# Norm scales on the weights, one norm fewer, the forget rows as a bias, and a re-planned state-space core in a four-layer decoder block

## The reference, cut to what matters

```
h = x
h = even_layer(h, mem)        # 8 heads differential attention, gated conv, 4 heads over mem
h = odd_layer(h, mem)         # 12 heads forgetting attention (C), 4 heads over mem (X)
h = h + s5_mixer(rms_norm(h, a_norm), ...);  h = h + conv_ffn(rms_norm(h, ffn_norm[0]), ...)
k, v = shared_kv(h, kv_norm, ...)            # rms_norm(h, kv_norm) @ w_kv
h = h + sb_mixer(rms_norm(h, b_norm), k, v, ...);  h = h + conv_ffn(rms_norm(h, ffn_norm[1]), ...)

def rms_norm(x, g):  return x * rsqrt(mean(x * x, -1) + EPS) * g
# forgetting attention, per head: s = q @ k.T * scale + cum[query] - cum[key], causal; softmax; @ v
#   cum = cumsum(log_sigmoid(u @ w_f + b_f)) per head
# s5_mixer: u = xn @ w_in; y = state-space scan of u; y = y + d_skip * u; gelu(y) @ w_glu, gated
```

## Time and profile before

| | |
|---|---|
| median of 3 runs | 2669.84 us (2668.22 to 2670.76) |
| the profiled execution, its own time | 2668.6 us |
| its span | 2666.8 us |
| mean granted TensorE clock | 0.944 of full speed |
| busy: PE, PEld, DVE, ACT, POOL | 2428.4 (91%), 1905.4 (71%), 1380.5 (52%), 921.4 (35%), 267.7 us (10%) |
| HBM read, written | 212.69 MB, 23.07 MB (88 GB/s) |

### The profile page before, as it was taken

How to read it: one execution, slowest core, us unless ns; L and a number is a source line. 1 busy time by engine, 2 the same in 40 slices (tenths; PEclk the granted TensorE clock), 3 DMA queues, 4 the chain that set the end, 5 groups by cost and what they waited for, 6 DMA issues and landing times.

```text
span 2666.8 us, 29121 instructions
## 1 busy us (share of the span) xinstructions
PE 2428.4 (91%) x10950; PEld 1905.4 (71%) x10950; DVE 1380.5 (52%) x2819; ACT 921.4 (35%) x1408; POOL 267.7 (10%) x314
## 2 busy tenths in 40 slices
PE   4789989799599999999889989999989899899998
PEld 3667667578477676766678768887868646688877
DVE  6875565746545353534454344444443585455543
ACT  3334434332443434342321332223333464322232
POOL 6541000024001010100000000000010231000000
PEclk9889999899799999999885999999989799899999
DMA  6344112125222121213263223332322101223222
GB/s 173 105 146 127 64 48 80 32 79 174 63 79 65 62 66 61 72 55 115 98 203 109 95 76 95 101 103 73 103 72 87 48 1 48 64 95 95 95 80 95
DMA packets 191360, 233.46 MB, mean 88 GB/s; under 512 B 39456, under 2 KB 120823, under 8 KB 191223
## 3 DMA queue, kind: packets, MB, share of 16 engines
q1 hardware_dynamic: 170503, 211.05, 24.9%
q10 hardware_dynamic: 20719, 20.56, 2.5%
HBM read 212.69 MB, written 23.07 MB: 88 GB/s over the span
## 4 chain that ended last, share of the span: by engine, by line
PE 84%; DVE 8%; issue 3%; ACT 3%; SPq 1%; DMA 1%; ACTq 0%; POOL 0%; DVEq 0%; POOLq 0%
PE G L1771 23%; PE G L1773 22%; PE G L1772 22%; PE X L1858 2%; PE X L1924 2%; PE X L1959 2%; PE X L1876 1%; ACT w_hi L991 1%; PE X L1829 1%; PE X L1780 1%; PE X L1843 1%; PE G L1866 1%; PE X L1846 1%; PE X L1817 1%; PE X L1842 1%
## 5 line engine op out<-in xcount | busy, mean ns | idle before, releaser
L1411 DVE TENSOR_TENSOR w_lo<-raw,w_hi 128x512 fp32r<-128x512 f32 x696 | 483.7, 737 | 606.4 <-ACT w_hi L991 606.1
L1771 PE MATMUL G<-w_hi,u_hi 128*128 128x512 f32 x1600 | 650.8, 407 | 21.9 <-issue 14.8
L1773 PE MATMUL G<-w_hi,u_lo 128*128 128x512 f32 x1600 | 632.0, 395 | 0.0
L1772 PE MATMUL G<-w_lo,u_hi 128*128 128x512 f32 x1600 | 631.3, 395 | 0.0
L991 ACT ACTIVATE w_hi<-raw 128x2048 fp32r<-128x2048 f32 (+1 forms) x176 | 333.8, 1897 | 825.4 <-PE G L1773 790.1
L1771 PE MATMUL G<-u_hi,w_hi 128*128 128x512 f32 x1120 | 450.5, 402 | 0.0
L1772 PE MATMUL G<-u_lo,w_hi 128*128 128x512 f32 x1120 | 441.6, 394 | 0.0
L1773 PE MATMUL G<-u_hi,w_lo 128*128 128x512 f32 x1120 | 441.0, 394 | 0.0
L1771 PEld LDWEIGHTS G<-w_hi,u_hi 128*128 128x128 f32 x1600 | 306.1, 191 | 106.6 <-issue 35.1
L1773 PEld LDWEIGHTS G<-w_hi,u_lo 128*128 128x128 f32 x1600 | 305.2, 191 | 66.8
L1772 PEld LDWEIGHTS G<-w_lo,u_hi 128*128 128x128 f32 x1600 | 306.0, 191 | 61.3 <-issue 0.5
(11 more groups left out here) (271 smaller groups left out, 2373.6 us busy)
## 6 DMA issues: line engine op xcount, KB each, us to landing
raw<-in_ffn_w_up SPq DMA_DIRECT2D x88, 512.0 KB, 4.7
raw<-in_e_w_in SPq DMA_DIRECT2D x56, 512.0 KB, 4.8
raw<-in_o_w_in SPq DMA_DIRECT2D x56, 512.0 KB, 4.6
raw<-in_ffn_w_down SPq DMA_DIRECT2D x40, 512.0 KB, 4.5
raw<-in_e_w_out SPq DMA_DIRECT2D x16, 512.0 KB, 4.6
raw<-in_o_w_out SPq DMA_DIRECT2D x16, 512.0 KB, 4.2
raw<-in_a_w_glu SPq DMA_DIRECT2D x16, 512.0 KB, 4.1
raw<-in_w_kv SPq DMA_DIRECT2D x16, 512.0 KB, 4.3
```

Source lines behind the costliest of these rows:

```text
L1411: V.tensor_tensor(w_lo[:, n % HL, k], raw[:, n % RAW, k], w_hi[:, n % HL, k].bitcast(F32), ALU.subtract).then_inc(w_lo_done, 1)
L1771: pe.matmul(out, lh, rh, start=start, stop=False)
L1772: pe.matmul(out, lh, rl, start=False, stop=False)
L1773: return pe.matmul(out, ll, rh, start=False, stop=stop)
```

## The change

1. **Scales on the weights.** For the 124 units behind a norm, `w_high` becomes four ACT instructions of 128x512 with a scale operand, each with its own count, and `w_low` four `scalar_tensor_tensor` instead of `tensor_tensor`, each waiting for its own piece. `u_hi` and `u_lo` lose the scale. The first `w_high` waits for the scale vectors. The 12 forget columns are multiplied by `o_norm` once.
2. **The second norm stage** (`b_norm`, `again=1`) is gone: the q chunks use the rows made for `kv_norm`.
3. **Forget rows.** `cum` is stored to DRAM once; each head's line is loaded back spread over 128 partitions into one of three buffers `c_row` (three loads by SP, nine by ACT, one behind the last exponential of a head). The matmul L1843 and DVE's `row` are gone. The query tiles run from i = 3 down to 0; before each, POOL sets the part of `c_row` above the diagonal to -3e38 (48 `affine_select` of 128x128), waiting for the maximum of the tile before; DVE's maximum reads `c_row` in place of `bias_tile` and waits for POOL.
4. **S5 core.** `d_skip` goes into the prepared matrices (32 small matmuls and 8 ACT copies more in `prep`), DVE's L1574 is gone. u and y are loaded back in pairs (72 transfers in place of 128), the scan has eight output buffers and y four, and the slots of V, Y, gelu and `u_lo` are re-planned.

```diff
-                nc.scalar.activation(w_hi[:, n % HL, 0:kn], raw[:, n % RAW, 0:kn], ACT.Copy).then_inc(w_hi_done, 1)
+                if unit_gain[n] is None:
+                    nc.scalar.activation(w_hi[:, n % HL, 0:kn], raw[:, n % RAW, 0:kn], ACT.Copy).then_inc(w_hi_done, 1)
+                    return
+                name, k0 = unit_gain[n]
+                for k in range(4):
+                    nc.scalar.activation(w_hi[:, n % HL, k], raw[:, n % RAW, k], ACT.Copy, scale=gain(name, k0 + k))\
+                        .then_inc(w_hi_done, 1)
...
+                        dve.wait_ge(w_hi_done, hi_before[n] + k + 1)
+                        V.scalar_tensor_tensor(w_lo[:, n % HL, k], raw[:, n % RAW, k], gain(name, k0 + k),
+                                               w_hi[:, n % HL, k].bitcast(F32), ALU.mult, ALU.subtract)\
+                            .then_inc(w_lo_done, 1)
...
-        plan_norm("h", "b_norm", again=1)
...
+            s.steps = [(hd, TT - 1 - i if kind == "C" else i) for hd in range(heads) for i in range(TT)]
...
+                if n == forget.n + 3:
+                    sp.wait_ge(*at_("cum_done", forget.i))
+                    sp.dma_start(dC, cum).then_inc(c_sum_stored, 16)
+                    sp.wait_ge(c_sum_stored, 16)
+                    for hd in range(3):
+                        sp.dma_start(c_row[hd], dC[hd].partition_broadcast(P)).then_inc(c_row_loaded[hd], 16)
...
+            def pool_c_rows(s, ts):
+                for t in ts:
+                    hd, i = s.steps[t]
+                    H = s.y0 + hd
+                    d = c_row[H % 3][:, P * i:P * i + P]
+                    if t % TT:
+                        pool.wait_ge(*at_("score", s.i, t - 1))
+                    else:
+                        pool.wait_ge(c_row_loaded[H % 3], 16 * (H // 3 + 1))
+                    pool.affine_select(out=d, in_=d, compare_op=ALU.is_ge, fill=BIG, base=0, pattern=[[-1, P]],
+                                       channel_multiplier=1).then_inc(*by("row_masked", s.i, t))
...
+                                dve.wait_ge(*at_("row_masked", s.i, t))
+                                b = c_row[head % 3][:, 0:L]
...
+                    if s.akind == "C" and is_last(s, t) and H < C_HEADS:
+                        act.dma_start(c_row[H % 3], dC[H].partition_broadcast(P)).then_inc(c_row_loaded[H % 3], 16)
...
-                            pe.matmul(b[:, 0:L], q, att[:, 4 + hd, 0:L], start=True, stop=False)
-                            ins = pe.matmul(b[:, 0:L], ones[0:C_HEADS, :], row[:, 0:L], start=False, stop=True)
+                            ins = pe.matmul(b[:, 0:L], q, att[:, 4 + hd, 0:L], start=True, stop=True)
...
-        S5_V = {2: 0, 3: 1, 4: 2, 5: 3, 7: 4, 8: 5, 9: 6, 10: 7}
-        S5_Y = {6: 0, 7: 1, 8: 2, 9: 3, 10: 4, 11: 5, 12: 6, 13: 7}
-        S5_SKIP = {9: (0,), 10: (1,), 11: (2,), 12: (3,), 13: (4,), 14: (5,), 15: (6, 7)}
-        S5_LOW = {10: (0,), 11: (1,), 12: (2, 3), 14: (4,), 15: (5, 6, 7)}
-        S5_GELU = {10: (0,), 11: (1,), 12: (2,), 13: (3,), 14: (4,), 15: (5, 6, 7)}
+        S5_V = {2: (0,), 3: (1,), 4: (2, 3), 7: (4, 5), 9: (6,), 10: (7,)}
+        S5_Y = {6: (0,), 7: (1,), 8: (2,), 9: (3,), 10: (4,), 11: (5, 6), 13: (7,)}
+        S5_GELU = {10: (0, 1), 11: (2, 3), 14: (4, 5), 15: (6, 7)}
+        S5_LOW = {9: (0, 1), 11: (2, 3), 14: (4, 5), 15: (6, 7)}
...
-                dve.wait_ge(s5_y_loaded[k], 16 * 8)
-                    y = big[:, 8 + k, :]
-                    V.scalar_tensor_tensor(y, big[:, k, :], gain("d_skip", k), y, ALU.mult, ALU.add)\
+                        ins = pe.matmul(b[0:32, g * P:g * P + 16], s5_skip[:, 32 * g:32 * g + 32], s5_fold,
+                                        start=False, stop=True)
```

More of the change, by code:

```diff
@@ L38, in weight_units @@
 def weight_units(w):
-    units = []
+    units, gains = [], []
     def cols(mat, k0, kn, c):
@@ L53, in paired, with chunk @@
                 (v[:, k0:k0 + 4, cb:cb + 256], slice(0, 4), slice(256, 512))]
-    def chunk(mat, c):
+    def chunk(mat, c, norm):
         units.append(cols(mat, 0, 4, c))
         units.append(cols(mat, 4, 4, c))
+        gains.extend([(norm, 0), (norm, 4)])
     def down(mat, kt, first=0):
@@ L95, in weight_units @@
                 units.append(paired(w["ffn_w_up"][layer], k0, DFF + 256 * c, 256 * c))
+                gains.append((f"ffn{layer}", k0))
         down(w["ffn_w_down"][layer], 22)
-    return units
+    return units, gains
 class Stage:
@@ L242, in stage, with plan_norm @@
             return s
[L244 to L251, removed]
+        def plan_norm(src, name, T=TT):
+            s = stage("norm", src=src, name=name, T=T, n=state["n"], h=state.get("h"), y=state.get("y"))
+            for t in range(T):
+                mark("squared", s.i, t)
+            for t in range(T):
+                mark("xn_ready", s.i, t)
             s.aux = [aux("u_ready", s.i, k) for k in range(KT)]
@@ L1110, in act_prep @@
                            .then_inc(s5_p_stored[c], 16)
+                if t == 0:
+                    nc.scalar.activation(s5_skip, ident[:, :], ACT.Copy, scale=gain("d_skip", 0))\
+                        .then_inc(*by("s5_skip", s.i, 0))
                 if t - 1 in PREP_K:
@@ L1118, in act_prep @@
                                          ACT.Copy).then_inc(*by("s5_evac", s.i, i, "k"))
+                    if i + 1 < KT:
+                        nc.scalar.activation(s5_skip, ident[:, :], ACT.Copy, scale=gain("d_skip", i + 1))\
+                            .then_inc(*by("s5_skip", s.i, i + 1))
                     act.wait_ge(*at_("s5_evac", s.i, i, "k"))
@@ L1481, in dve_slot @@
                         .then_inc(*by("score", s.i, t))
-                    if s.akind == "C" and i == TT - 1 and hd < s.heads - 1:
-                        V.tensor_scalar(row, cum, ident[0:C_HEADS, head + 1:head + 2], None, ALU.mult)\
-                            .then_inc(*by("row_ready", s.i, hd + 1))
                 if 1 <= t <= T:
@@ L1619, in _ @@
                         dve.wait_ge(*at_("u_hi_done", s.i, k))
-                        V.scalar_tensor_tensor(u_lo[:, k, 0:P * s.T], X[:, s.aux[k] % 4, 0:P * s.T], gain(s.name, k),
-                                               u_hi[:, k, 0:P * s.T].bitcast(F32), ALU.mult, ALU.subtract)\
+                        V.tensor_tensor(u_lo[:, k, 0:P * s.T], X[:, s.aux[k] % 4, 0:P * s.T],
+                                        u_hi[:, k, 0:P * s.T].bitcast(F32), ALU.subtract)\
                             .then_inc(*by("u_ready", s.i, k))
```

204 lines of the change are left out of this document (106 added, 98 removed).

## The result

The changed kernel takes 2596.16 us (median of 4 runs, 2591.71 to 2603.32) against 2670.3 beside it: a ratio of 0.973, with a 95% interval from 0.970 to 0.975. That is 74 us less. I had forecast 2624.5 with 2600 as the low end: the sign was right, and the gain was 1.6 times as large as forecast and outside the range. The profiled execution was the fastest of the four, 2591.71 us with a span of 2589.5, so span against span the gain is 77.3 us.

The account below looks back on a forecast made before the run. PE, busy 91% of the span, was taken to bound the kernel. The terms summed to -45.1 us, taking the profiled 2668.6 to 2623.5, as a median 2624.7, stated as 2624.5 us; range 2600 to 2642.

Parts of the forecast that it names:

- Part 1: Forgetting attention: without the row matmul its streaming goes, -25.8 us over 12 heads, with +2.5 back in the last group.
- Part 2: Start of each group of forgetting attention: PE's three waits for DVE's `row` go, -6.2 us, and clock loss behind, -3.4.
- Part 3: Second norm: PE's gap between the v chunk and the q chunk goes, -7.2 us, nothing reasonable less than -5.
- Part 4: Weights' split: ACT's longer w_high ahead of eight norms +4.9, PE's waits for DVE -7.2, unscaled u_hi and u_lo -3 us.
- The rival in which part 1 turns into waiting for DVE: Forgetting attention: DVE or the mask loop takes the row matmul's 26 us as waiting; 2650 us, chance 0.05.
- Part 5: Prep: 32 more small matmuls and slower w_lo, less two waits for w_hi; net +1.8 us (-2 to +7).
- Part 7: POOL's 48 masks in forgetting attention: wait hidden, but they run beside DVE's w_lo; +1.5 us (0 to +15).
- Part 6: S5 core: re-planned slots remove one PE wait and lengthen another; -3 us in all (-30 with the clock, to +15).
- rival of stalling pairs: S5 core: u and y of a pair wait for the second tile's store; +15 us, 2639.5, chance 0.10.
- The wait of 4.8: S5 core: PE's second wait for ACT's copy, as ACT stood in gelu(0) needing y0 from DRAM; 4.8 us, to go.
- the first wait: S5 core: PE waits 3.2 us for ACT, which splits a weight unit before copying Y1; stays, +1.7 us.
- the first rival: S5 core: with fewer pauses the clock stays at 2.4 GHz; -20 us, 2604.5, chance 0.12.

## Why the prediction was too small

- **Part 1, the row matmul: the step that failed.** "The other 0.19 I take for the change to the next kind of operand, which stays when q*k stands there instead." It does not stay. The 0.19 belongs to the row matmul's 12 operand rows and goes with it, and so do 0.1 us ahead of it and 0.1 us behind it that the chain of waits had put down to its neighbours: 0.41 us in each of 48 slots, 19.7 us, of the 32 by which the spans moved more than forecast. I had -34.9 as the bound if the 0.19 went too; the true value, 44.6, lies outside even that, since I only looked at what the chain put on the row's own line. The streaming (25.8 forecast, 0.21 us per 128 keys) was right. Of the 2.5 us given back in the last group 1.3 came, and elsewhere: the waits for DVE's scaling there are 4.2 us instead of 4.4, and a wait ahead of a product of the down product is 3.6 instead of 2.1.
- **Part 2** held for the waits (6.2, all gone). Taking the wait away alone gave 6.6 us by the medians, where I had 9.6 with the clock; in forgetting attention itself the traces give 9.7, with two falls of the clock of 1.6 us each.
- **Part 3**: the gap of 7.2 was right. The 2 to 3 us of clock behind it are not shown to belong to the part.
- **Part 4**: the pieces cost each norm 0.6 us, as forecast, and of the waits that I listed 6.1 went, of 7.2 (9.9 + 2.6 to 5.9 + 0.5). Against them stand 2.1 more that I had not listed, for the rows that PE transposes ahead of attention (30.5 to 32.6). The norms without a scale on `u_hi` (0.60 us each, not 0.69) are 0.2 to 0.3 us shorter from the first transpose to the first product in the four of layers 3 and 4; I had 3 us for all eight, and 1.7 came in seven of them; in the eighth, the first of the even layer, the same stretch grew from 15.7 to 16.6. What was missed is that parts 1 and 4 lean on each other. Without the pieces, the shorter slots of part 1 let PE wait 18.1 us for DVE, not 9.9, and the pieces take that away. By the times they are worth 21.8 us in the changed kernel and 15.7 alone, but the intervals leave that difference of 6 open; the waits are what shows it. The rival in which part 1 turns into waiting for DVE (2650, chance 0.05) is real to the extent of these 8 us, and part 4 is what stopped it.
- **Part 5**: first slot of memory attention 201.6 before, 204.1 after: +2.5, forecast +1.8. **Part 7**: nothing on PE, forecast +1.5; DVE loses 0.1 us beside a mask.
- **Part 6**: 6.8 us against 3 in this trace, but the stretch takes 100.1 to 103.9 us in nine traces with this core (107.1 before, 105.7 to 109.3 in four with the old one). The three longest are the ones in which PE waits for a load of u (6.0, 5.4 and 0.7 us), which no trace of the old core has: my rival of stalling pairs came in some executions. The wait of 4.8 is gone; the first wait, which I had growing by 1.7, grew by 0.3 (3.2 to 3.5). The core still runs at the lower clock, as forecast against the first rival (1338 to 1395 us):

```profile
1338.00:1395.00 57.00, 57.00 (x315) 54.49 (x315) 20.01 (x34) 11.79 (x19) 0.00 (x0) 0.51 0.47 127
```

By the sum: 19.7 us of the operand height, 3.8 in the S5 core and 2.8 behind the second norm are 26 of the 32 us missing; the last two are of the size by which executions differ. The other 6 are spread: 3 in forgetting attention (4.0 are left of 54.8 when 44.6 and 6.2 are taken off, where I had 3.4 of clock less 2.5 given back), the rest in terms of 1 to 3 us. Between the medians 29 us are missing, not 32, since the execution traced was the fastest.

By the Trainium skill (GPSIMD Engine Reference, Key points), GpSimd shares its SBUF interfaces with the vector engine, and some instructions of the latter contend with it. I priced the worst of it at all the time that the masks last. The traces have DVE's scaling of 128x512 at 0.61 us beside a mask and at 0.49 in the kernel before, 0.12 us for a mask where the worst was 0.64. Cutting the masks from 128 columns to one left the time as it was (2597.23 against 2596.16): DVE has slack here.

## What to carry to other kernels

A matmul costs more than its columns when its operand has another number of rows than its neighbours: price it from the start of the matmul ahead of it to the second one behind it, not from its own line. When an edit shortens the engine that sets the pace, list which waits of that engine were hidden by what is taken away, and check whether another part of the same change covers them. And where an engine does look-ahead work just before a stage that hangs on it, put the look-ahead behind the stage's first step: that gave 18 us more here. A difference of 2 or 3 us in one stretch of one trace needs a second trace before it gets a cause.

## What the hardware showed that I had not expected

A matmul of 64 operand rows between ones of 128 pays the same 0.38 us as one of 12 rows, and one of 128 pays nothing (2.34, 2.33, 1.95 us from q*k to the second product). Over the same 26 us of work the granted clock was 0.54 to 0.74 in different traces, and none of the edits here explains it. One GpSimd mask of 128x128 took 0.36 to 0.40 us as a mean in forgetting attention (0.29 as a median) and 0.64 in differential attention, and one of a single column still 0.19.
